# Encoder trunk, dilated attention: the second head group's queries stored in four runs of every fourth token instead of in token order

## The reference, cut to what matters

```python
B_GROUPS = ((128, 1), (512, 4), (2048, 16))

def apply_rope(x, pos):
    ...
    x1, x2, rest = x[..., :half], x[..., half:ROPE_DIMS], x[..., ROPE_DIMS:]
    return jnp.concatenate([x1 * cos - x2 * sin, x2 * cos + x1 * sin, rest], axis=-1)

def mixer_b(q, k, v, pos):
    q, k = apply_rope(q, pos), apply_rope(k, pos)
    outs, lses = [], []
    for g, (window, dil) in enumerate(B_GROUPS):
        qg = q[:, g * MIX_HEADS:(g + 1) * MIX_HEADS]
        o, lse = band_attention(dilate(qg, dil)[..., None, :, :], dilate(k, dil), dilate(v, dil),
                                window // (2 * dil), return_lse=True)
        ...
    wts = jax.nn.softmax(jnp.stack(lses), axis=0)
    o = jnp.einsum('gbhl,gbhld->bhld', wts, jnp.stack(outs).astype(jnp.float32))
```

## Time and profile before

| | |
|---|---|
| median of 3 runs | 2143.52 us (2143.46 to 2143.62) |
| the profiled execution | 2141.04 us, its span 2139.2 us |
| granted TensorE clock, mean | 0.996 |
| TensorE matmul busy | 2100.8 us (98%) |
| VectorE busy | 1607.0 us (75%) |
| ScalarE busy | 1066.6 us (50%) |

### The profile page before, as it was taken

How to read it: one execution, slowest core, us unless ns; L and a number is a source line. 1 busy time by engine, 2 the same in 40 slices (tenths; PEclk the granted TensorE clock), 3 DMA queues, 4 the chain that set the end, 5 groups by cost and what they waited for, 6 DMA issues and landing times.

```text
span 2139.2 us, 31770 instructions
## 1 busy us (share of the span) xinstructions
PE 2100.8 (98%) x10880; PEld 1766.5 (83%) x10880; DVE 1607.0 (75%) x3674; ACT 1066.6 (50%) x2625; POOL 16.2 (1%) x23
## 2 busy tenths in 40 slices
PE   8999999999999997999999999999999999999998
PEld 8888888888888886788888888888888888888886
DVE  6777878777655468868888888888888888677465
ACT  5444444545554232456555555555565565665321
POOL 0000000000000000000000000000000000000001
PEclk9999999999999999999999999999999999999999
DMA  8311111111127451213233133143233232325652
GB/s 268 107 45 36 54 56 50 60 60 55 40 89 241 151 180 55 70 54 95 62 98 90 52 103 100 51 109 86 65 110 85 65 108 72 104 60 182 213 166 85
DMA packets 242458, 204.99 MB, mean 96 GB/s; under 512 B 20852, under 2 KB 198076, under 8 KB 242300
## 3 DMA queue, kind: packets, MB, share of 16 engines
q1 hardware_dynamic: 242300, 202.97, 31.4%
HBM read 168.40 MB, written 34.52 MB: 95 GB/s over the span
## 4 chain that ended last, share of the span: by engine, by line
PE 75%; DVE 14%; DMA 5%; issue 3%; ACT 2%; SPq 0%; POOL 0%; DVEq 0%; POOLq 0%; ACTq 0%
PE bank L1131 14%; PE bank L1133 14%; PE bank L1132 14%; PE bank L1209 7%; PE bank L1181 7%; DVE work L1573 6%; PE bank L1301 5%; PE bank L1303 5%; PE bank L1302 5%; PE bank L1195 3%; DMA work<-weight_scratch 2%; DVE ring L1573 2%; DMA weight_scratch<-trig 2%; DVE work L1669 1%; DVE work L1717 1%
## 5 line engine op out<-in xcount | busy, mean ns | idle before, releaser
L1131 PE MATMUL bank<-x_ops,ring 128*128 128x512 f32 (+1 forms) x1808 | 843.6, 467 | 14.1 <-issue 11.8
L1133 PE MATMUL bank<-x_ops,ring 128*128 128x512 f32 (+1 forms) x1808 | 698.5, 386 | 0.0
L1132 PE MATMUL bank<-x_ops,ring 128*128 128x512 f32 (+1 forms) x1808 | 696.6, 385 | 0.0
L1573 DVE SCALAR_TENSOR_TENSOR ring<-raw,ring 128x512 fp32r<-128x512 f32 x368 | 251.5, 685 | 216.7 <-ACT ring L1340 216.6
L1133 PEld LDWEIGHTS bank<-x_ops,ring 128*128 128x128 f32 x1808 | 340.9, 189 | 71.1
L1131 PEld LDWEIGHTS bank<-x_ops,ring 128*128 128x128 f32 x1808 | 345.3, 191 | 58.3 <-issue 12.5
L1401 ACT COPY work<-bank 128x256 f32<-128x256 f32 (+2 forms) x448 | 164.4, 367 | 430.5 <-PE bank L1195 429.7
L1132 PEld LDWEIGHTS bank<-x_ops,ring 128*128 128x128 f32 x1808 | 345.2, 191 | 37.5
L1340 ACT CAST ring<-raw 128x512 fp32r<-128x512 f32 x368 | 226.9, 618 | 167.0 <-PE bank L1303 146.9
L1209 PEld LDWEIGHTS bank<-work 128*128 128x128 f32 x1744 | 262.2, 190 | 44.4 <-ACT work L1401 3.8
L1418 ACT ACTIVATE work<-work,soft 128x256 f32<-128x256 f32 (+2 forms) x448 | 226.5, 506 | 134.8 <-DVE soft L1717 133.1
(11 more groups left out here) (77 smaller groups left out, 2161.8 us busy)
## 6 DMA issues: line engine op xcount, KB each, us to landing
raw<-in_w_in_b SPq DMA_DIRECT2D x160, 256.0 KB, 3.1
raw<-in_w_out SPq DMA_DIRECT2D x112, 256.0 KB, 3.4
raw<-in_w_in_a SPq DMA_DIRECT2D x80, 256.0 KB, 3.1
work<-weight_scratch SPq DMA_DIRECT2D x24, 768.0 KB, 5.3
y_scratch<-work SPq DMA_DIRECT2D x32, 512.0 KB, 2.7
x_ops<-y_scratch SPq DMA_DIRECT2D x64, 256.0 KB, 4.8
work<-v_scratch SPq DMA_DIRECT2D x48, 256.0 KB, 4.4
raw<-in_w_mkv SPq DMA_DIRECT2D x32, 256.0 KB, 5.3
```

What stands on the lines that cost most here:

```text
L1131: nc.tensor.matmul(dst, w_h, x_h, start=start, stop=False, skip_group_check=again)
L1132: nc.tensor.matmul(dst, w_h, x_l, start=False, stop=False, skip_group_check=again)
L1133: return nc.tensor.matmul(dst, w_l, x_h, start=False, stop=stop, skip_group_check=again)
L1573: return nc.vector.scalar_tensor_tensor(out=dst, in0=a, scalar=1.0, in1=b, op0=ALU.mult, op1=op)
```

## The change

Group 1's queries get `order=4` beside their rot: they are stored in four runs of every fourth token, as the keys are. `pieces` and `views` learn to do both at once, the shuffled copy `turned` is viewed piece by piece, and the score tiles of group 1 now take 128 neighbouring elements.

```diff
@@ class Dest
     def pieces(self, h):
 
         first = h * HALF
-        if self.order > 1 or first >= self.rot:
+        if first >= self.rot:
             return [(first - self.rot, first, HALF)]
         return [(0, self.rot, HALF - self.rot), (L - self.rot, 0, self.rot)]
 
     def views(self, h, parts=P):
 
         buf = self.buf[0:parts, :]
-        if self.order > 1:
-            d, n = self.order, HALF // self.order
-            return [(buf.rearrange("p (r n) -> p r n", r=d)[:, :, h * n:(h + 1) * n],
-                     lambda v: v.rearrange("p (n r) -> p r n", r=d))]
+        d = self.order
 
         def taker(a, n):
+            if d > 1:
+                return lambda v: v[:, a:a + n].rearrange("p (n r) -> p r n", r=d)
             return lambda v: v[:, a:a + n]
 
+        if d > 1:
+            runs = buf.rearrange("p (r n) -> p r n", r=d)
+            return [(runs[:, :, at // d:(at + n) // d], taker(t - h * HALF, n))
+                    for at, t, n in self.pieces(h)]
         return [(buf[:, at:at + n], taker(t - h * HALF, n)) for at, t, n in self.pieces(h)]
@@ pairs of layer 1
             add_pair(w_in_b[0], b_col(0, i), Dest(b_q[0], "q", rot=W_B),
-                     b_col(1, i), Dest(b_q[1], "q", rot=4 * W_B))
+                     b_col(1, i), Dest(b_q[1], "q", rot=4 * W_B, order=4))
@@ b_tiles, g == 1
-                qd = dilated(q, 4)
+                qd = q.rearrange("p (r n) -> p r n", r=4)
@@ turned_views
             if dest.order > 1:
-                return [(b.rearrange("p (r n) -> p r n", r=dest.order), dest.views(h, ROPE)[0][1])]
+                return [(b[:, t - h * HALF:t - h * HALF + n].rearrange("p (r n) -> p r n", r=dest.order),
+                         take) for (_, t, n), (_, take) in zip(dest.pieces(h), dest.views(h, ROPE))]
```

## The result

The changed kernel takes 2154.39 us, the median of 6 runs (2152.01 to 2156.18), against 2143.49 us for the kernel before on the same chip (6 runs, 2141.7 to 2146.32). The ratio is 1.005 (95% interval 1.0037 to 1.0063): 10.9 us slower. I had said slower, and 2159.3 us, inside 2151 to 2168. So the sign and the mechanism have to be tested as much as the 4.9 us that are missing.

What follows compares the result with a forecast made beforehand. TensorE's own work was taken to bound the kernel, except where VectorE's unbroken stretch holds it in pair c. Eleven heads times 1.56 us, 17.2, less 1.4 for loads, added 15.8 to 2143.5: 2159.3 us, range 2151 to 2168.

Steps and rivals of the forecast that it cites:

- Rotary embedding: VectorE's multiplications of group 1's queries by the table, now read every fourth element: 1.56 us more per head.
- Evictions: ScalarE's and VectorE's strided PSUM reads cost nothing; strided `r5` costs 0 to 0.39 us, hidden by idle time in pair a.
- Score tiles: TensorE's loads of group 1's queries get shorter, mostly hidden under matmuls: a saving of some 1.4 us in all.
- rival price: In TensorE's score tile loads: if the whole 122 ns came back each time, 11.7 us would be saved.
- both: Rival: TensorE's loads come back whole and VectorE's rotation is hidden too, the only way to faster, 2131.8 us; chance 0.02.
- How often: The rotation's price is paid in pair c in eleven heads; the first head's rotation counts as free.
- Absorbed: Rival: VectorE's idle 1.49 us before the split takes the added 1.56, leaving only the saving, 2142.1 us; chance 0.07.
- loads whole: Rival: the price of TensorE's strided loads is not hidden and 11.7 us return, giving 2149 us; chance 0.06.
- twice: Rival: late weights or mixing make the score tiles' waits grow another 1.56 us in eleven heads, 2176.5 us; chance 0.03.
- `r5` on the path: Rival: VectorE's strided read of `r5` in pair a is slow and uncovered, 4.3 us more, 2163.6 us; chance 0.07.

Runs made afterwards that it cites:

- the half in order: Changed kernel with only half h=0 of group 1's queries reading the tables in order (wrong angles): 2152.72 us, ratio 1.0051 to the kernel before.
- the first: Changed kernel with group 1's queries reading the cosine and sine tables in order (wrong angles): 2141.49 us, ratio 0.9995 to the kernel before.
- the pair with tables in runs: Changed kernel and kernel before, both with a second table copy in four runs and value reads at step 20 instead of 14: 2137.7 and 2137.96 us.
- the reads behind: Value reads issued at step 20 of pair c, not 14: kernel before 2133.55 us (0.9955), changed 2150.65, changed with table in order 2133.28 (0.9958).
- its own run: Changed kernel with half h=1 of group 1's queries adding neighbouring elements of `r5` (wrong ones): 2154.36 us, ratio 1.0056 to the kernel before.

## Why the prediction was right in kind and too high by five

**Rotary embedding.** Right, and the tests leave it no rival. I had 1.56 us per head from the keys' rows; the unbroken stretch grew by 1.61. The runs of 64 are neither free nor dearer, and the price goes with the elements: the half in order took half of the wait away. The place was right too: the idle 1.49 us absorbed nothing. The wait didn't stay one of 1.9 us, as I had said; it is 0.63, 0.44 and 1.25 us at three loads, 2.32 of idle time in PEld, while TensorE's matmuls lose 1.59. A wait's total is not what TensorE loses.

**Evictions.** Reads of PSUM cost nothing. `r5` costs its upper bound, 0.36 of 0.39, and the idle time behind it takes all of it: 2.18 there before, 1.79 now. VectorE's growth of 24.9 us is the 19 and 4.7 of my two sums, and 1.2 more.

**Score tiles.** The loads became 189 ns and TensorE's steps with them shorter by 1.7 us in all, as forecast (1.4). But I counted this as a gain, and it is none: the saved time runs into the next wait, L1213 for L1405 in pair a, 0.21 us a head before (at 1268.56), 0.40 after. That costs 2.4. My rival price was wrong by half as well: a tile has two such loads, not one (the earlier trace rows has 16 for eight tiles), so 122 ns back on each would be 23.4 us in 96 tiles and not 11.7. Loads coming back whole would then have made the kernel 6.2 us faster with the rotation's price paid, and "both" was not the only way to faster. The ledger's 1.7 rules out either size. Three comparisons with the table in order agree: the layout's own worth was a ratio of 0.9995 in the first, 0.3 us in the pair with tables in runs, and 0.9958 against 0.9955 with the reads behind. Zero, within what can be told.

**How often.** Eleven heads and the same place in each, right. The first head's rotation was not free: waits grew there by 0.8 us in the ledger.

**The step that failed** is the sentence that the weights' way is late by the same 1.56 us as TensorE, so that "the score tiles' waits in pair a don't grow". They didn't grow; they shrank. I had treated the weights' way as a chain of fixed length that starts later. It isn't: its first link, a write of 12 KB, is issued into four reads of 256 KB each, which were issued at a step of TensorE's and not at a time of VectorE's. Late enough, it misses part of them. The row that should have told me was there to be read: SP waiting 46.8 us for twelve such writes. With the reads moved away in both kernels the difference is 17.1 us, and 10.9 without. The term for this was nothing, and it measured 6.2 us. With it beside my 17.2 for the rotation, the loads at nothing and the first head at 0.8, the sum is 11.8; that is no test of the account, since the 6.2 was made with the 10.9. What tests it is that the relief goes when the reads are moved, in the time and in the ledger. That the forecast was only 4.9 us off has some luck in it: the relief of 6.2 was left out, but so was the first head's 0.8, and the loads were counted with 1.4 that never came.

The split of the 10.9 us into its terms rests on one profiled execution each, 14.6 apart, where the medians are 10.9 apart. Which execution falls where I can't say; the kernels with the reads behind scatter less, so the weights' way is a part of it. That the write is slow *because* of the reads is shown by moving the reads alone. They are issued on one queue; whether they contend there or in DRAM stays open.

**The rivals.** Absorbed, loads whole, both, and twice are ruled out by the waits above; `r5` on the path by its own run.

## What to carry to other kernels

Before you store an operand in another order, list every instruction that now reads or writes against the grain, and price the ones on the engine that is late, not those on the engine that you want to help: the loads got faster and it was worth nothing. A delay on one engine can move a transfer out of another's way, so look at what a queue waits for on both sides of a late instruction; here the reads that stood in the way were worth as much (10 us) as the whole change cost. And when a wait is taken away, read the next one on the same engine before you count the gain.

## What the runs showed of the hardware

- One operand in SBUF read every fourth float32 element slows a VectorE instruction of 32x512 from 0.61 to 1.01 us from start to start, although the other operand is in order. It does so too where the other operand is in PSUM: 1.04 against 0.68 us at 128x512. Group 2's queries, stored with order 16, read every sixteenth, and their multiplication takes no longer (at 1007.89 above, 0.98 us from start to start). The Trainium skill (Advanced Engine Details and Errata, Memory Cachelines) says that a line of 16 bytes needs at least two hits, which neither stride gives; these rows agree. The Trainium skill's other figure, that one can stride four float32 elements for free (SBUF — State Buffer, the note on cachelines under Door 1: The DMA port swizzle), does not agree with them.
- Reading PSUM every fourth element cost ScalarE and VectorE nothing: 0.59 against 0.58 us and 0.69 against 0.67 at 128x512, and ScalarE's 24 evictions of 128x256 have a mean of 381 ns in both kernels.
- TensorE's weight load reads every fourth float32 element in 311 ns and neighbouring ones in 189, and it is nearly all hidden: 1.7 us over 96 tiles is 0.018 us a tile of two loads.
- VectorE pauses 0.1 us (0.70 from start to start in place of 0.60) where an instruction's partitions start elsewhere, at 32 or 64, than those of the one ahead of it.
- A write of 12 KB to DRAM issued 1.3 to 1.7 us behind reads of 1 MB in all kept SP waiting 3.9 us on average, and 1.0 with those reads out of the way.
